# Two layers of attention and retention: w_b ahead of w_a, retention rows turned by way of HBM

## The reference

```
h = rmsnorm(x, g_mix);  z = h @ w_in           # 1024 -> 5888 columns
aq, ak, av, rq, rk, rv, rg, ga, gb = split(z)
ya = window_attention(rope(aq), rope(ak), av, sinks) @ w_a      # 512 -> 1024, 8 heads of 64
r  = chunkwise_retention(rot(rq), rot(rk), rv)                  # 4 heads, 256 values each
r  = r * rsqrt(mean(r*r) + eps) * silu(rg)
yb = r @ w_b                                                    # 1024 -> 1024
x  = x + (sigmoid(ga) * ya + sigmoid(gb) * yb) @ w_out
x  = x + square(relu(rmsnorm(x, g_mlp) @ w_up)) @ w_down
```

## Time and profile before

| | |
|---|---|
| median of three runs | 1015.1 us |
| the profiled execution | 1015.0 us |
| its span, first to last instruction | 1013.1 us |
| TensorE busy | 1004.5 us, 99% |
| VectorE, ScalarE busy | 720.8 us, 502.3 us |
| mean granted TensorE clock | 0.998 |

### The profile page before, as it was taken

One profiled execution on the slowest core, in us unless ns is written; L12 is line 12 of the kernel. 1 busy time (PEld: TensorE's weight loads), 2 busy tenths in 40 slices (PEclk: granted clock), 3 DMA queues, 4 the chain that ended last, 5 costly groups with the idle time before them and its releaser, 6 DMA issues.

```text
span 1013.1 us, 13575 instructions
## 1 busy us (share of the span) xinstructions
PE 1004.5 (99%) x5653; PEld 850.0 (84%) x5653; DVE 720.8 (71%) x817; ACT 502.3 (50%) x616; POOL 170.7 (17%) x129
## 2 busy tenths in 40 slices
PE   9999999999999999999999999999999999999997
PEld 8887788888888888887788888888887899899796
DVE  5878656766565665787765667888877757789974
ACT  6544554454444545454554454444468545654352
POOL 0520000000000000430000020000000149169730
PEclk9999999999999999999999999999999999999999
DMA  9797444555556455596553557555554754345451
GB/s 341 250 288 246 160 155 142 170 180 191 199 176 207 166 178 175 187 294 225 166 167 125 169 147 283 201 177 209 204 170 135 238 178 167 125 166 141 121 188 41
DMA packets 103644, 188.60 MB, mean 186 GB/s; under 512 B 9160, under 2 KB 18464, under 8 KB 103456
## 3 DMA queue, kind: packets, MB, share of 16 engines
q1 hardware_dynamic: 103408, 187.66, 55.8%
q10 hardware_dynamic: 176, 0.09, 0.0%
HBM read 180.69 MB, written 4.72 MB: 183 GB/s over the span
## 4 chain that ended last, share of the span: by engine, by line
PE 93%; DVE 3%; DMA 1%; issue 1%; ACT 1%; SPq 0%; DVEq 0%; ACTq 0%
PE bank L786 13%; PE bank L789 12%; PE bank L788 12%; PE bank L1091 11%; PE bank L811 8%; PE bank L815 7%; PE bank L822 7%; PE bank L1095 6%; PE bank L1173 2%; DVE w_lo L1873 2%; PE bank L984 1%; PE bank L1397 1%; PE bank L968 1%; DMA a_bounce<-arena 1%; PE bank L793 1%; PE bank L803 1%
## 5 line engine op out<-in xcount | busy, mean ns | idle before, releaser
L1873 DVE TENSOR_TENSOR w_lo<-arena,w_hi 128x2048 fp32r<-128x2048 f32 (+1 forms) x80 | 185.1, 2323 | 95.2 <-ACT w_hi L1485 94.8
L1873 DVE TENSOR_TENSOR w_lo<-raw,w_hi 128x2048 fp32r<-128x2048 f32 (+1 forms) x78 | 181.1, 2331 | 80.1 <-ACT w_hi L1485 80.0
L1485 ACT ACTIVATE w_hi<-raw 128x2048 fp32r<-128x2048 f32 (+1 forms) x83 | 157.1, 1892 | 102.3 <-PE bank L789 71.4
L1485 ACT ACTIVATE w_hi<-arena 128x2048 fp32r<-128x2048 f32 (+1 forms) x80 | 151.3, 1892 | 104.6 <-PE bank L789 80.8
L1091 PE MATMUL bank<-hT,w_hi 128*128 128x512 f32 x504 | 123.4, 391 | 0.0
L786 PE MATMUL bank<-w_hi,hT 128*128 128x512 f32 (+1 forms) x296 | 114.1, 385 | 0.9 <-issue 0.9
L1091 PEld LDWEIGHTS bank<-hT,w_hi 128*128 128x128 f32 x504 | 92.2, 188 | 17.6
L2482 POOL TENSOR_TENSOR rstd<-mean,const 128x1 f32<-128x1 f32 (+1 forms) x16 | 9.1, 579 | 528.5 <-DVE mean L1882 359.4
L789 PE MATMUL bank<-w_hi,hT 128*128 128x512 f32 (+1 forms) x256 | 97.9, 382 | 0.0
L788 PE MATMUL bank<-w_lo,hT 128*128 128x512 f32 (+1 forms) x256 | 97.9, 382 | 0.0
L811 PE MATMUL bank<-w_hi,hT 128*128 128x512 f32 (+1 forms) x216 | 83.3, 388 | 0.7 <-DVE arena L2131 0.7
(11 more groups left out here) (342 smaller groups left out, 1886.7 us busy)
## 6 DMA issues: line engine op xcount, KB each, us to landing
arena<-in_w_in SPq DMA_DIRECT2D x22, 1024.0 KB, 5.3
raw<-in_w_in SPq DMA_DIRECT2D x20, 1024.0 KB, 5.3
arena<-in_w_up SPq DMA_DIRECT2D x16, 1024.0 KB, 5.3
raw<-in_w_up SPq DMA_DIRECT2D x16, 1024.0 KB, 5.3
arena<-in_w_down SPq DMA_DIRECT2D x16, 1024.0 KB, 5.1
raw<-in_w_down SPq DMA_DIRECT2D x16, 1024.0 KB, 5.1
raw<-in_e_w_in SPq DMA_DIRECT2D x6, 1024.0 KB, 5.1
arena<-in_e_w_in SPq DMA_DIRECT2D x6, 1024.0 KB, 5.1
```

What stands on the lines that cost most here:

```text
L1485: act.activation(w_hi[:, p % SPLIT_RING, :, 0:n], raw_at(p)[:, :, 0:n], copy).then_inc(hi_ready, 1)
L1873: dve.tensor_tensor(w_lo[:, s, :, 0:n], raw_at(p)[:, :, 0:n], w_hi[:, s, :, 0:n].bitcast(F32), ALU.subtract).then_inc(lo_ready, 1)
```

## The change

Five things, in both layers:

1. The retention output of tile 0 moves to window 6, of tile 1 to window 7 (banks 2, 5 and 4, 3). Squares, mean, root and product follow them there.
2. Attention goes one group later: scores in windows 7 to 10, probabilities 8 to 11, values 9 to 12. Window 12 is new and stands between the two halves of w_b. The attention output has tiles of its own, `o_hi` and `o_lo`.
3. VectorE writes the retention rows with permuted columns. SP stores them to `h_bounce`, fetches them in blocks, VectorE turns the blocks into `r_rows`, ScalarE copies them to `uT_hi`, VectorE subtracts to `uT_lo`. The 16 transposes on TensorE and `turn_hi`, `turn_lo` for them are gone.
4. w_b comes ahead of w_a, its rows loaded as "(p k)" in place of "(k p)", to fit the permuted rows.
5. The transpose of the attention blocks on VectorE (`aT`) stands at group 7 in place of 6.

The core of the diff. SyncE's queue:

```diff
+                if piece == 23:
+                    for t in range(T):
+                        sp.wait_ge(r_ready, 2 * l + t + 1)
+                        store_rows(h_bounce[t * P:(t + 1) * P, :], h[:, t, :], h_stored)
...
+                for c in range(2):
+                    for half in range(2):
+                        load(row_blocks_piece(ins["w_b"][l], c, half))
+                        if c == half == 0:
+                            sp.wait_ge(h_stored, 16 * T * (l + 1))
+                            fetch_blocks(h_moved, h_bounce, h_blocks)
                 for c in range(2):
                     load(square_piece(ins["w_a"][l], c, 0))
-                for w in ("w_b", "w_out"):
+                for c in range(2):
+                    for half in range(2):
+                        load(square_piece(ins["w_out"][l], c, half))
```

TensorE, after the groups:

```diff
+                pe.wait_ge(r_hi, l + 1)
+                pe.wait_ge(r_lo, l + 1)
+                for c in range(2):
+                    tokens_out(l * USES + USE_YB + c, l * PIECES + PIECE_B + 2 * c, 2, uT_hi, uT_lo)
+                    if c == 0:
+                        window(l, W_IN_GROUPS)
                 pe.wait_ge(oT_lo, PAIRS * (l + 1))
-                tokens_out(l * USES + USE_YA, l * PIECES + PIECE_A, 1, uT_hi, uT_lo)
+                tokens_out(l * USES + USE_YA, l * PIECES + PIECE_A, 1, o_hi, o_lo)
...
-                turn_rows(h, lambda t: r_ready, lambda t, i: 2 * l + t + 1)
-                for c in range(2):
-                    tokens_out(l * USES + USE_YB + c, l * PIECES + PIECE_B + 2 * c, 2, hT_hi, hT_lo,
-                               turn=4 * l + 1 if c == 0 else None)
```

ScalarE, in the loop over groups:

```diff
                     window(l, g - 1)
+                    if g == W_IN_GROUPS - 1:
+                        act.wait_ge(r_turned, l + 1)
+                        act.activation(uT_hi[:, :, :], r_rows, copy).then_inc(r_hi, 1)
                     if g != RQ:
                         step(p + 2 * g + 1)
```

VectorE, in the loop over groups, ahead of step(p + 2 * g):

```diff
-                    if g == 6:
+                    if g == SCORES_AT:
                         dve.wait_ge(a_blocks, 16 * T * BLOCKS * (l + 1))
                         turn_blocks(aT, a_moved, A_SLOTS).then_inc(aT_ready, 1)
...
+                    if g == W_IN_GROUPS - 1:
+                        dve.wait_ge(h_blocks, 16 * BLOCKS * (l + 1))
+                        turn_blocks(r_rows, h_moved, KD).then_inc(r_turned, 1)
```

VectorE, after the loop:

```diff
+                dve.wait_ge(r_hi, l + 1)
+                dve.tensor_tensor(uT_lo[:, :, :], r_rows, uT_hi[:, :, :].bitcast(F32), ALU.subtract).then_inc(r_lo, 1)
                 window(l, W_IN_GROUPS - 1)
```

VectorE, in window 7:

```diff
+                if g == 7:
+                    retention_rows(l, 0)
+                if SCORES_AT <= g < SCORES_AT + PAIRS:
+                    softmax(l, g - SCORES_AT, between=(lambda: retention_mean(l, 1)) if g == 7 else lambda: None)
+                if g == 7:
+                    retention_rows(l, 1)
```

The product that writes the permuted rows:

```diff
-                    src = bank[:, ((6, 7), (4, 3))[t][hd // 2], (hd % 2) * RET_V:(hd % 2 + 1) * RET_V]
-                    last = dve.scalar_tensor_tensor(out=h[:, t, at], in0=src, scalar=ret_rstd[:, t, hd:hd + 1],
-                                                    in1=z_rg[:, t, at], op0=ALU.mult, op1=ALU.mult)
+                    src = bank[:, RET_BANKS[t][hd // 2], (hd % 2) * RET_V:(hd % 2 + 1) * RET_V]
+                    last = dve.scalar_tensor_tensor(out=h[:, t, at].rearrange("p (s f) -> p f s", f=BLOCK),
+                                                    in0=src.rearrange("p (f s) -> p f s", f=BLOCK), scalar=ret_rstd[:, t, hd:hd + 1],
+                                                    in1=z_rg[:, t, at].rearrange("p (f s) -> p f s", f=BLOCK),
+                                                    op0=ALU.mult, op1=ALU.mult)
```

More of the change, by code:

```diff
@@ L112 @@
     0, 16, 32, 48, 64, 68, 72, 80, 84, 88)
+PHASES = 3
+X_PHASE, M_PHASE, MLP_PHASE = range(PHASES)
 KEPT_TABLES = ("ident", "minus_half", "odd_group_row", "odd_group_state", "stacked_eye")
@@ L428, in build_program @@
         r_ready = sem("r_ready")
+        h_stored = sem("h_stored")
+        h_blocks = sem("h_blocks")
+        r_turned = sem("r_turned")
+        r_hi = sem("r_hi")
+        r_lo = sem("r_lo")
         m_ready = sem("m_ready")
@@ L1022, in window @@
                     last.then_inc(s_far_done, 1)
-                    pe.wait_ge(aT_ready, l + 1)
-                if 6 <= g < 6 + PAIRS:
-                    i = g - 6
+                    for hd in range(RET_HEADS):
+                        last = pe.matmul(bank[:, RET_BANKS[0][hd // 2], (hd % 2) * RET_V:(hd % 2 + 1) * RET_V],
+                                         s_ret[:, 0, hd * P:(hd + 1) * P], z_rv[:, 0, hd * RET_V:(hd + 1) * RET_V],
+                                         start=True, stop=True)
+                    last.then_inc(ret_done, 1)
+                if SCORES_AT <= g < SCORES_AT + PAIRS:
+                    i = g - SCORES_AT
                     n = l * PAIRS + i
+                    if i == 0:
+                        pe.wait_ge(aT_ready, l + 1)
                     if n:
@@ L1035, in window @@
                     last.then_inc(scores_done, 1)
-                if g == 10:
-                    pe.wait_ge(scores_read, l * PAIRS + PAIRS)
+                if g == 7:
+                    pe.wait_ge(s_far_ready, l + 1)
                     for hd in range(RET_HEADS):
-                        last = pe.matmul(bank[:, 6 + hd // 2, (hd % 2) * RET_V:(hd % 2 + 1) * RET_V],
-                                         s_ret[:, 0, hd * P:(hd + 1) * P], z_rv[:, 0, hd * RET_V:(hd + 1) * RET_V],
-                                         start=True, stop=True)
+                        dst = bank[:, RET_BANKS[1][hd // 2], (hd % 2) * RET_V:(hd % 2 + 1) * RET_V]
+                        pe.matmul(dst, s_ret[:, 1, hd * P:(hd + 1) * P], z_rv[:, 1, hd * RET_V:(hd + 1) * RET_V],
+                                  start=True, stop=False)
+                        last = pe.matmul(dst, s_far[:, hd * P:(hd + 1) * P], z_rv[:, 0, hd * RET_V:(hd + 1) * RET_V],
+                                         start=False, stop=True)
                     last.then_inc(ret_done, 1)
-                if 7 <= g < 7 + PAIRS:
-                    n = l * PAIRS + g - 7
+                if PROBS_AT <= g < PROBS_AT + PAIRS:
+                    n = l * PAIRS + g - PROBS_AT
                     pe.wait_ge(probs_ready, n + 1)
-                    if g > 7:
+                    if g == PROBS_AT:
+                        pe.wait_ge(r_ready, 2 * l + 1)
+                    else:
                         pe.wait_ge(probsT_even, n)
@@ L1058, in window @@
                     if i == 0:
-                        pe.wait_ge(s_far_ready, l + 1)
+                        pe.wait_ge(r_ready, 2 * l + T)
                     else:
@@ L1068, in window @@
                     last.then_inc(pv_done, 1)
[L1069 to L1078, removed]
             def mlp_up(l, f):
@@ L1568, in window @@
                     act.activation(probsT[:, 0, :], bank[:, 2, 0:384], copy).then_inc(probsT_even, 1)
-                if 8 <= g < 8 + PAIRS:
-                    i = g - 8
+                if VALUES_AT <= g < VALUES_AT + PAIRS:
+                    i = g - VALUES_AT
                     act.wait_ge(pv_done, l * PAIRS + i + 1)
-                    act.activation(uT_hi[:, i, :], bank[:, 3, 0:SEQ], copy).then_inc(oT_hi, 1)
-                if 6 <= g < 6 + PAIRS:
-                    n = l * PAIRS + g - 6
+                    act.activation(o_hi[:, i, :], bank[:, 3, 0:SEQ], copy).then_inc(oT_hi, 1)
+                if g in (6, 7):
+                    t = g - 6
+                    act.wait_ge(ret_done, 2 * l + t + 1)
+                    for hd in range(RET_HEADS):
+                        src = bank[:, RET_BANKS[t][hd // 2], (hd % 2) * RET_V:(hd % 2 + 1) * RET_V]
+                        last = act.activation(h[:, t, hd * RET_V:(hd + 1) * RET_V], src, ACT.Square,
+                                              accum_out=ret_ss[:, t, hd:hd + 1])
+                    last.then_inc(ret_sq, 1)
+                if SCORES_AT <= g < SCORES_AT + PAIRS:
+                    n = l * PAIRS + g - SCORES_AT
                     act.wait_ge(top_ready, n + 1)
@@ L1639, in _ @@
                 if l:
-                    turn_hi(4 * l, gain=V_MIX + KD * l)
+                    turn_hi(PHASES * l + X_PHASE, gain=V_MIX + KD * l)
                     for t in range(T):
@@ L1650, in _ @@
                 window(l, W_IN_GROUPS - 1)
[L1651 to L1654, removed]
+                step(p + PIECE_B)
+                step(p + PIECE_B + 1)
+                window(l, W_IN_GROUPS)
+                for i in range(2, 4):
                     step(p + PIECE_B + i)
-                turn_hi(4 * l + 2, scale=0.5)
+                for i in range(2):
+                    step(p + PIECE_A + i)
+                turn_hi(PHASES * l + M_PHASE, scale=0.5)
                 for c in range(2):
@@ L1660, in _ @@
                     if c == 1:
```

(19 more changed lines are left out.)

96 lines of the change are left out of this document (45 added, 51 removed).

## The result

The changed kernel takes 1020.36 us (median of four runs, 1019.70 to 1021.23), the kernel before 1015.18 in the same comparison. The ratio is 1.0051, 95% interval 1.0038 to 1.0063: slower by 0.5% (5.2 us). The profiled execution took 1020.46 us with a span of 1018.7.

The account below looks back on a forecast made before the run. TensorE's queue, busy 99% of the span, was taken as the bound. 1015.0 - 5.0 - 0.7 + 0.4 + 7.5 gave 1017.2 us at full clock; one clock fall of 1.7 made 1018.9, 8 in 10 range 1016.0 to 1021.8.

Parts of the forecast that it names:

- the pause: TensorE idle before the first w_b matmul, waiting for uT_lo: 3.74 us a layer, 7.5 in all.
- the clock: After a pause TensorE's clock falls to 1.2 GHz: 0.5 to 2.8 us a fall, 1.7 taken, one fall counted.
- my sum at full clock: Whole kernel, all terms without a clock fall: +2.2 us, 1017.2; bounds given as 1016.2 to 1018.3.
- The chain: Window 10 on: block transpose, split, exponentials, uT_hi, hi(25), lo(25), uT_lo, then w_b starts at W+18.82.
- What left TensorE: Between w_a and w_b: 16 transposes and the wait behind them removed, 2.49 us a layer, 5.0 in all.
- the wait for the gate product: Group 8 waiting for VectorE's gate product: gone once the first pair's softmax moves to window 7, 0.7 us won.
- rival A: Pause before w_b, clock falls in at least one layer: 1018.9 with one fall, 1020.6 with two; chance 0.52.
- Rival B: Pause before w_b, but the clock stays: 1017.2; chance 0.31.
- The last pause of the trace before: At the old kernel's end the clock fell 2.2 us after the last matmul; taken as evidence for a fall.
- rival C: h blocks reach VectorE's block transpose late: 5 us late would give 1027; slack 9 us; chance 0.07.
- The strided product: VectorE's retention products with strided writes: 1.66 us for four, perhaps doubled, making lo(19) 3 us later; free either way.
- Rival D: No real pause before w_b, uT_lo ready without hi(25) and lo(25) in front: faster, 1009.7; chance 0.10.

Follow-up runs that it names:

- experiment 1: Changed kernel with VectorE's uT_lo subtraction moved ahead of lo(25), the split of w_b's second piece: 1009.18 us, ratio 0.9941 to the kernel before.
- experiment 2: Changed kernel with ScalarE's uT_hi copy moved ahead of window 10's exponentials, VectorE's order unchanged: 1014.94 us, ratio 0.9993 to the kernel before.
- experiment 7: Kernel of experiment 1 plus eight fillers (sixteen 128-column matmuls, result unread) ahead of w_a in each layer: 1012.76 us, ratio 0.9975.
- experiment 6: Changed kernel plus 15 fillers (128-column float32 matmuls, result unread) in TensorE's pause ahead of its wait for r_hi: 1016.48 us, ratio 1.0011.
- experiment 8: Kernel of experiment 1 with VectorE's retention product written contiguously, without the column permutation (computes another product, time only): 1009.27 us, ratio 0.9940.

## Why the prediction was right, step by step

I predicted 1018.9 (1016.0 to 1021.8), slower, with the pause and the fallen clock as the likeliest course. It is that course, 1.5 us above the point. Part of that nearness is luck, for two terms were too small and lie on opposite sides of the sum: the clock took 3.9 us where I had 1.7, and the change saves 6.2 us (experiment 1) where my terms come to 5.3. (The lower bound of my sum at full clock is 1016.1, not 1016.2; nothing hangs on it.)

- **The pause** was predicted at 3.74 us a layer and is 3.63 and 3.62 in the list of waits; from start to start, as the prediction counts, it is 3.71 in the first layer (w_b would have started at 151.38 + 0.80, and starts at 155.89). The chain came as worked out: window 10 starts at W = 137.16, uT_hi at W+10.40 (predicted 10.43), hi(25) at W+12.20 (12.24), lo(25) at W+14.13 (14.17), uT_lo at W+16.34 (16.38), w_b at W+18.73 (18.82). Experiment 1 shows lo(25) in front of uT_lo to be enough for it, experiment 2 that ScalarE's order holds 1.7 us of it.
- **What left TensorE** was 2.49 + 0.35 - 0.2 = 2.64 us a layer by my terms. With the pause away the stretch takes 116.76 us in the profile of experiment 1 (70.36 to 187.12) against 119.70: 2.94. Of the 2.49, experiment 7 gives 1.8 to the sixteen transposes, if a filler's matmul stands for a transpose, and so 0.7 to the wait behind them. Most of the remaining 0.3 is the wait for the gate product, which I took from its listed idle time (0.35 a layer). From start to start it cost more. First window 7 before, then window 8 of experiment 1, which holds the same matmuls:

```profile
95.09 0.49 PE L1031 MATMUL bank<-arena 64*128 64x128 f32 x4
95.41 0.60 PE L1033 MATMUL bank<-arena 64*128 64x256 f32 x4
95.94 0.88 PE L1051 MATMUL bank<-const,arena 128*128 128x128 f32 x6
```

```profile
112.07 0.49 PE L1067 MATMUL bank<-arena 64*128 64x128 f32 x4
112.39 0.60 PE L1069 MATMUL bank<-arena 64*128 64x256 f32 x4
112.92 0.88 PE L1091 MATMUL bank<-const,arena 128*128 128x128 f32 x6
113.55 0.47 PE L841 MATMUL bank<-w_hi,hT 128*128 128x512 f32 x1
```

  Before, the next group starts 2.01 us after the window does (95.09 to 97.10), in experiment 1 1.48 (112.07 to 113.55): 0.53 saved where the profile lists 0.28 idle. Idle is counted from the end of the matmul before, and that end lies behind the next start when nothing waits. This is read from traces; no run takes that wait away alone.
- **The clock** is the term that was mis-sized. I took one fall at 1.7 us. Both layers fell in the profiled execution, at 2.6 and 1.5 us, and experiment 6 puts 3.9 us on them together. So the number of falls was wrong by one, and the middle price a little low. A term for each pause (two at 1.7) would have given 1020.6, and that case stood in the text as the second half of rival A; I chose the lower one. Rival B (no fall) would have been 1016.5 by experiment 6, near its 1017.2. The last pause of the trace before was a fair guide to whether the clock falls, and to when in one layer only: its clock fell 2.2 us after the last matmul, here it fell 2.7 us after in the first layer, but 4.5 us after in the second (539.60 to 544.08), when w_b was running again. So my argument that part of the low time passes while TensorE still waits held in the first layer (0.9 us of 6.8) and not in the second.
- **The Trainium skill** ("TensorE: Matmul & The Clock Gate", section "Why this matters for your kernels") warns that an idle gap between matmul bursts lets the clock fall. The trace agrees for the pauses of 3.6 us. The gap from which the page warns is longer than 1.9 us, and there the measurement decides: in experiment 2 the clock fell after a gap of 1.9 us in one layer of the profiled execution.
- **The blocks** were not late (rival C):

```profile
113.19 0.98 SPq L688 DMA_DIRECT2D h_bounce<-h_sb x2
115.97 0.38 SPq L683 DMA_DIRECT2D raw<-in_w_b x1
121.70 1.80 SPq L694 DMA_DIRECT2D arena<-h_bounce x4
```

  Stores at 113.2 (predicted 113), fetches from 121.7 to 123.5, landed a median of 5.9 us later, so near 129 as predicted, and VectorE takes them at 137.87 without a wait.
- **The strided product** takes 0.675 us each in place of 0.476, 2.20 for four: inside the bounds I gave it (up to double), and hidden, as experiment 8 shows.
- **Rival D** (no pause, faster) named what it would need: uT_lo without hi(25) and lo(25) in front. It priced that at 1009.7. Experiment 1 is that kernel, 1009.2. Only lo(25) has to give way.

So the change does save what it could: 6.2 us by experiment 1. It gave back 7.3 us by a hand-over in the wrong place in one queue, and another 3.9 by the clock that the pause let fall. The kernel of experiment 1 beats both.

## What to carry to other kernels

When work moves off the bound engine, its last result becomes a wait of that engine: write down what stands ahead of the producing instruction in its own queue, and put the producer ahead of everything that is needed later than it. Price a pause of TensorE with the clock as well, once for every pause: here the clock added half as much again to pauses of 3.6 us, and it fell after one of two pauses of 1.9 us. And a filler in TensorE's queue tells a pause's own price from the clock's in one run.

## What the hardware showed that I had not expected

- A pause of 1.9 us can let the granted clock fall and need not: two equal pauses of one execution did the one and the other, and ten runs spread over 3.1 us where the kernel of experiment 1, without them, spreads over 1.2 in five.
- The clock can fall after work has begun again. In the second layer TensorE restarts at 543.22 and the level falls about 0.9 us later, 4.5 us after the pause began. The low level then lasted 3.4 us. In the first layer it lasted 6.8, though TensorE had work all the time from 155.89 on.
- A float32 matmul of identity by identity, 128 columns, runs as two of 0.112 us; a transpose of the same tile is one of about the same length (sixteen transposes take 1.91 us with the last one's own time, the sixteen matmuls of eight fillers 1.95 in experiment 7).
